# A hybrid encoder layer on one core: the moving operand of the last matmul stages in blocks of 512 columns, softmax by two heads a step

## What is computed

```python
D_MODEL = SEQ = 1024; BATCH = DEPTH = 1; N_MEM = 256; GROUP = 256; XATTN_HEADS = 4   # head width 256
def memory_cross_attention(h, mem_n, wq, wk, wv, wo):
    q = (h @ wq).reshape(B, T, XATTN_HEADS, XATTN_HEAD_DIM)
    k = (mem_n @ wk).reshape(B, M, XATTN_HEADS, XATTN_HEAD_DIM)
    v = (mem_n @ wv).reshape(B, M, XATTN_HEADS, XATTN_HEAD_DIM)
    s = jnp.einsum('bthd,bmhd->bhtm', q, k).astype(jnp.float32) * (XATTN_HEAD_DIM ** -0.5)
    p = jax.nn.softmax(s, axis=-1).astype(h.dtype)
    o = jnp.einsum('bhtm,bmhd->bthd', p, v).reshape(B, T, D_MODEL)
    return o @ wo
def reference(x, mem, ...):
        h = rms_norm(x, norm_mix[l])
        p = h @ w_in[l]                                   # 1024 -> 3904 columns
        p_a, p_b, p_c, p_d = jnp.split(p, splits, axis=-1)
        y_a = rwkv7_mixer(...)                            # delta-rule recurrence
        y_b = conformer_conv_mixer(...)                   # causal depthwise convolution, width 31
        y_c = hgrn2_mixer(...)                            # gated linear recurrence
        y_d = stick_breaking_mixer(...)                   # causal attention without softmax
        y = jnp.concatenate([y_a, y_b, y_c, y_d], axis=-1).astype(x.dtype)
        x = x + y @ w_out[l]
        hx = rms_norm(x, norm_xattn[l])
        mn = rms_norm(mem, norm_mem[l])
        x = x + memory_cross_attention(hx, mn, ...)
    return rms_norm(x, norm_final)
```

## Time and profile before

| | us |
|---|---|
| median of 3 runs | 1131.08 |
| lowest, highest | 1128.71, 1133.42 |
| span of the profiled execution, first to last instruction | 1128.3 |
| PE busy in it | 1058.6 (94%) |
| wide stages of the tail, first to last matmul | 822.5 to 1122.1 |
| of these, from the third block of the out projection on | 874.9 to 1122.1 |

### The profile page before, as it was taken

How to read it: one execution, slowest core, us unless ns; L and a number is a source line. 1 busy time by engine, 2 the same in 40 slices (tenths; PEclk the granted TensorE clock), 3 DMA queues, 4 the chain that set the end, 5 groups by cost and what they waited for, 6 DMA issues and landing times.

```text
span 1128.3 us, 25035 instructions
## 1 busy us (share of the span) xinstructions
PE 1058.6 (94%) x10748; PEld 915.3 (81%) x10748; DVE 576.8 (51%) x837; ACT 415.1 (37%) x719; POOL 288.5 (26%) x259
## 2 busy tenths in 40 slices
PE   6999978999899899989989799999989999999997
PEld 5788866886688698768868678888579999999997
DVE  6316998864447734153584875333231175445115
ACT  7314102023644411365534635555530062223033
POOL 3334640011326100113402000451142433422220
PEclk9999989999999999989989899999999999999999
DMA  7111110000111100021100017665551101111104
GB/s 236 36 31 47 47 47 3 3 22 20 30 28 47 29 4 3 2 75 39 39 20 20 2 42 216 200 186 163 193 180 38 48 31 46 58 47 39 38 20 150
DMA packets 83999, 71.16 MB, mean 63 GB/s; under 512 B 4081, under 2 KB 72881, under 8 KB 83890
## 3 DMA queue, kind: packets, MB, share of 16 engines
q1 hardware_dynamic: 83890, 69.57, 20.4%
HBM read 56.97 MB, written 12.58 MB: 62 GB/s over the span
## 4 chain that ended last, share of the span: by engine, by line
PE 69%; DVE 18%; ACT 7%; DMA 2%; issue 2%; POOL 1%; SPq 0%; DVEq 0%; ACTq 0%; POOLq 0%
PE units L1103 10%; PE bank L1372 7%; PE bank L1371 7%; PE bank L1373 7%; PE bank L1052 7%; PE bank L1054 6%; PE bank L1053 6%; DVE yT L1676 5%; PE bank L1092 5%; DVE A L1673 3%; ACT A L1392 2%; ACT B L1392 2%; PE duo L1319 2%; DVE late L1676 1%; PE duo L990 1%
## 5 line engine op out<-in xcount | busy, mean ns | idle before, releaser
L1371 PE MATMUL bank<-vhi,act_hi 128*128 128x256 f32 x704 | 200.4, 285 | 0.0
L1372 PE MATMUL bank<-vlo,act_hi 128*128 128x256 f32 x704 | 199.4, 283 | 0.0
L1373 PE MATMUL bank<-vhi,act_lo 128*128 128x256 f32 x704 | 198.1, 281 | 0.0
L1052 PE MATMUL bank<-act_hi,whi 128*128 128x512 f32 x464 | 192.7, 415 | 0.0
L1054 PE MATMUL bank<-act_hi,wlo 128*128 128x512 f32 x464 | 182.8, 394 | 0.0
L1053 PE MATMUL bank<-act_lo,whi 128*128 128x512 f32 x464 | 182.8, 394 | 0.0
L1103 PEld LDWEIGHTS units<-A 64*64 64x64 f32 x4608 | 147.1, 139 | 36.4 <-issue 18.3
L1103 PE MATMUL units<-A 64*64 64x64 f32 x4608 | 155.4, 224 | 22.3 <-DVE A L1839 9.7
L975 POOL TENSOR_SCALAR whi<-wraw 128x512 fp32r<-128x512 f32 x62 | 57.1, 922 | 456.5 <-PE bank L1054 388.4
L1372 PEld LDWEIGHTS bank<-vlo,act_hi 128*128 128x128 f32 x704 | 134.8, 192 | 0.0
L1373 PEld LDWEIGHTS bank<-vhi,act_lo 128*128 128x128 f32 x704 | 134.8, 191 | 0.0
(11 more groups left out here) (186 smaller groups left out, 1593.3 us busy)
## 6 DMA issues: line engine op xcount, KB each, us to landing
wraw<-in_w_in SPq DMA_DIRECT2D x62, 256.0 KB, 2.8
A<-in_x SPq DMA_DIRECT2D x8, 512.0 KB, 7.4
x<-in_x SPq DMA_DIRECT2D x8, 512.0 KB, 7.8
moved<-in_wq SPq DMA_DIRECT2D x16, 256.0 KB, 4.4
keys_dram<-moved SPq DMA_DIRECT2D x16, 256.0 KB, 2.1
vals_dram<-moved SPq DMA_DIRECT2D x16, 256.0 KB, 3.9
vraw<-in_w_out SPq DMA_DIRECT2D x16, 256.0 KB, 3.1
vraw<-keys_dram SPq DMA_DIRECT2D x16, 256.0 KB, 2.6
```

The costliest lines, as they stand in the source:

```text
L1052: mm(bank, wh, act_hi[:, k, cols], start=k == 0, stop=False)
L1371: mm(bank, ah, vhi[:, (m + 1) % 2, k, :], start=k == 0, stop=False)
L1372: mm(bank, ah, wide_lo(m)[:, k, :], start=False, stop=False)
L1373: ins = mm(bank, al, vhi[:, (m + 1) % 2, k, :], start=False, stop=k == KT - 1)
```

## The change

**The order of the mixers** is no longer planned. `mixer_order()` reads it from two tables, `TILE_ORDER` (the order of the projection's tiles) and `MERGE` (a string that says which chain moves next and how many steps). On every engine the instructions up to the sixteenth wide stage are the same ones in the same order as before; only the tail differs.

**The blocks of the wide stages** stand in a table `WIDES`. The out projection keeps two blocks of 256 columns and then has one of 512; scores and values have two of 512 each. A 512-column stage is again 24 matmuls, each with a moving operand of 128x512, and fills a whole bank. There are 56 wide stages in place of 96. Chunks are still 256 KB and 48 in number, but in a 512-column block one chunk is one slice k (128 rows of 2 KB), so a block takes 8.

**Places of the split operand.** The 512-column block of `o` lies in `o_rest`, on the memory of `yT`; POOL may write it once all eight `ysplit` are done. The four blocks of `s` and `f` go round 12 places of one slice each: eight in `vhi`/`vlo`, four in `vmore`, which lies on `ysp`. So the first four slices of a block have places of their own, and the last four take the places of slices of the block before. For these PE counts a new semaphore `v_used` in the last stage (i = 7) of a block, after slices 1, 3 and 5; POOL waits for it.

**Softmax** takes two heads a step: one maximum over 128x2x256, two exponentials, one reciprocal of two values, two multiplications. The final norm's two parts are 512 and 512 columns in place of 768 and 256.

```diff
+WIDES = (("o", 0, 0, 256), ("o", 1, 256, 256), ("o", 2, 512, 512),
+         ("s", 0, 0, 512), ("s", 1, 512, 512), ("f", 0, 0, 512), ("f", 1, 512, 512))
+WIDE_LOADS = [(m, k, HALF // w) for m, (_, _, _, w) in enumerate(WIDES) for k in range(0, KT, HALF // w)]
-IDLE = 24.099
...
+    for turn in MERGE.split():
...
-    s += [("wide", "o", n, i) for n in range(3) for i in range(2 if n < 2 else 0, TT)]
+    s += [("wide", "o", n, i) for n in range(2) for i in range(2, TT)]
     for i in range(TT):
-        s.append(("wide", "o", 3, i))
+        s.append(("wide", "o", 2, i))
         if i > 1:
             s.append(("hT", i - 2))
         s.append(("x2n", i))
-    for n in range(4):
+    for n in range(2):
         for i in range(TT):
             s += [("wide", "s", n, i), ("smax", n, i)]
...
-                pj.plan((name,) + a, reads=2 if a[0] == "s" else 1)
+                pj.plan((name,) + a, reads=3 if a[0] == "s" else 1)
...
+            if name == "o":
+                return o_rest[:, k, 0, :], o_rest[:, k, 1, :]
+            slot = (8 * (m - wide_at["s", 0]) + k) % 12
+            if slot >= 8:
+                return vmore[:, 0, slot - 8, :], vmore[:, 1, slot - 8, :]
+            return vhi[:, slot, :], (vlo0, vlo1)[slot // 4][:, slot % 4, :]
+
+        def wait_wide_place(eng, m, k):
...
+            elif name == "o" and n == 2 and k == 0:
+                eng.wait_ge(sem("y_split"), TT)
+            elif (name, n, k) == ("s", 0, 0):
+                pj.rd_open(eng, ("wide", "o", 1, TT - 1))
+            elif (name, n, k) == ("s", 1, 0):
+                pj.rd_open(eng, ("wide", "o", 2, 1))
+            elif name == "f" or (name, n) == ("s", 1) and k >= 4:
+                before = 8 * (m - wide_at["s", 0]) + k - 12
+                first, at = divmod(before, 8)
+                if at >= 6:
+                    pj.rd_open(eng, ("wide",) + WIDES[wide_at["s", 0] + first][:2] + (TT - 1,))
+                else:
+                    eng.wait_ge(sem("v_used"), 3 * first + at // 2 + 1)
...
-                bank = pj.pe_open(pe, key)[:, 0:256]
+                bank = pj.pe_open(pe, key)[:, 0:w]
                 for k in range(KT):
-                    if i == 0 and k % 2 == 0:
-                        pe.wait_ge(sem("v_split"), 4 * m + k // 2 + 1)
+                    if i == 0 and k % (HALF // w) == 0:
+                        pe.wait_ge(sem("v_split"), first + k // (HALF // w) + 1)
                     ah, al = hi[:, k, :], lo[:, k, :]
...
+                    mm(bank, ah, bh, start=k == 0, stop=False)
+                    mm(bank, ah, bl, start=False, stop=False)
+                    ins = mm(bank, al, bh, start=False, stop=k == KT - 1)
+                    if name != "o" and i == TT - 1 and k % 2 and k < KT - 1:
+                        ins.then_inc(sem("v_used"), 1)
```

More of the change, by code:

```diff
@@ L125, in mixer_chains, with step, halves @@
 def mixer_chains():
-    rec, stick, conv = [], [], []
+    rec, conv, stick = [], [], []
     def proj(*kind):
         return ("proj",) + kind + (1,)
-    def step(chain, stage, parts, *waits):
-        chain.append((stage, parts, ([chain[-1][0]] if chain else []) + list(waits)))
-    def halves(chain, stage, parts, waits=lambda h: None):
-        before = [chain[-1][0]]
+    def step(chain, stage, *needs):
+        chain.append((stage, ([chain[-1][0]] if chain else []) + list(needs)))
+    def halves(chain, stage, needs):
@@ L185, in mixer_chains @@
[L185 to L191 removed]
+            halves(rec, ("hlev", i, l), lambda h: [("hlev", i, l - 1, h) if l else ("hgate", i)])
@@ L211, in mixer_chains @@
                 if u:
[L212 removed]
+                    stick.append((("sbv", i, th, u - 1), [("sbt", i, th, u - 1)]))
                 if u < n:
[L214 to L225 removed]
@@ new lines, in mixer_chains, with cut @@
+                    stick.append((("sbt", i, th, u), [("sbz", i, th, u)]))
+            step(stick, ("sbo", i, th), proj("s", i, "gate"))
+    for i in range(2):
+        step(stick, ("ysplit", i), ("rfin", 1), ("hfin", 1), ("cfin",))
+    mem = [(("mn", 0), [("rfin", 1)]), (("mn", 1), []), (("mT", 0), [("mn", 0)]), (("mT", 1), [("mn", 1)])]
+    def cut(chain, *firsts):
+        at = [0] + [n for n, (stage, _) in enumerate(chain) if stage in firsts] + [len(chain)]
+        return [chain[a:b] for a, b in zip(at, at[1:])]
@@ new lines, in mixer_chains, with put @@
+    first, second, h0, h1 = cut(rec, ("lora", 1), ("hgate", 0), ("hgate", 1))
+    s0, s1 = cut(stick, ("sv", 1))
+    return {"a": first, "b": second, "g": h0, "h": h1, "c": conv, "s": s0, "t": s1, "m": mem}
+def mixer_order():
+    chains = mixer_chains()
+    pieces = [(t, 3, k) for t in (("xw",), FIRST_TILE) for k in range(KT)]
+    pieces += [(t, h, k) for t in TILE_ORDER for h, k in piece_list(t)]
+    order, placed = [], set()
+    def put(stage, needs=()):
+        assert all(n in placed for n in needs), (stage, needs)
+        order.append(stage)
+        placed.add(stage)
+    for turn in MERGE.split():
+        for _ in range(int(turn[1:] or 1)):
+            if turn[0] != "p":
+                put(*chains[turn[0]].pop(0))
+                continue
+            kind, h, k = pieces.pop(0)
+            put(("piece" if h < 2 else "part",) + kind + (h, k))
+            if k == max(piece_list(kind))[1]:
+                put(("proj",) + kind + (min(h, 1),))
+    assert not pieces and not any(chains.values())
@@ L931, in _ @@
                 sem("gain_loaded"), 16)
-            load_wides(2, 12)
+            for u in range(8, len(WIDE_LOADS)):
+                load_wide(u)
             for i in range(TT):
```

400 lines of the change are left out of this document (117 added, 283 removed), and 23 rows, old and new, of tables (MERGE, TILE_ORDER, TILE_RANK).

## The result

| | before | after |
|---|---|---|
| median (lowest to highest) of the runs taken together, us | 1132.33 (1128.71 to 1133.42) | 1124.11 (1122.31 to 1126.10), 5 runs |
| ratio, with its 95% interval | | 0.9939 (0.9918 to 0.9959) |
| span of the profiled execution | 1128.3 | 1120.5 |
| first 512-column stage, start | 874.85 | 876.29 |
| from there to the last matmul ("the tail" below) | 247.22 | 237.60 |

One run of before that lay far off (1940 us) is left out of the range; it is one of the five behind the median, which without it is 1131.7. Two later measurements of the same changed kernel gave 1121.73 us (8 runs) and 1122.05 us (6 runs). All 19 runs together have a median of 1122.4 us, and 52 runs of before, from all the comparisons of this study and without the one of 1940 us, 1132.5 us.

What follows compares the result with a forecast made beforehand. PE was taken to bound the kernel; -12.8 (matmuls) - 3.3 (stalls) + 0.6 (supply) + 0.3 (end) = -15.2 us carried the median of 1131.08 to 1115.9 us. Range 1112.5 to 1120, to 1122 with one slow boundary.

Steps and rivals of the forecast that it cites:

- The bound and the part that doesn't change: Whole kernel: PE alone sets the tail's end at clock 1.00; the 875 us before it keep their time.
- Matmuls, -12.8: Tail: 1920 matmuls of 256 columns become 960 of 512 at 0.2267 us each, 12.8 us less.
- the rival that the fixed part is not halved: Tail matmuls: the 13 ns are not tied to the instruction, pairing saves nothing, 1128.7 us; chance 0.05.
- Stalls at the transposes, -3.3: Out projection's normalized rows: PE's two waits at transposing groups go away, 3.3 us less.
- Supply, +0.6: Second scores and second values blocks: PE waits 0.3 us at each for late slices, 0.6 us more.
- The prediction's bound: Supply at three boundaries: with splits of up to 2.14 us a chunk, up to about 10 us more.
- POOL falls behind at one boundary: One block boundary: slow splits cost PE 3.4 us and a lower clock 1.7, giving 1121.0 us; chance 0.07.
- the lower clock it had feared: Behind a PE wait for POOL: 1.2 GHz for 3.4 us, costing 1.7 us, part of the slow boundary rival.
- Banks, clock, end: Tail: no waits for scores banks, clock 1.00 throughout, DVE's last addition 0.3 us longer.
- The rival of a lower clock in dense work: Tail: denser column feeding lowers PE's clock; 45 us at 1.2 GHz give 1138 us; chance 0.03.
- The sum: Whole kernel: -12.8 - 3.3 + 0.6 + 0.3 = -15.2 us, giving 1115.9 us.
- The stated range: Whole kernel's time: 1112.5 to 1120 us, reaching to 1122 with one slow boundary and holding some 0.85.

Runs made afterwards that it cites:

- align256_deep: Changed kernel with pads of 256 bytes, giving all operands the remainder 128 modulo 256, and four landing buffers in place of two; 1117.29 us, ratio 0.9848 to the kernel before.
- the best kernel: The kernel `align256_deep`: pads of 256 bytes and four landing buffers added to the changed kernel; 1117.29 us, tail 232.24 us.
- shift: Changed kernel with 96 more already met wait instructions at the start of PE's program, to move instruction fetches against the loads; 1128.92 us (one run).
- misalign: Changed kernel with the pad of 32 bytes moved in front of `vhi`, so `vhi` and `vlo0` get remainder 160 too; 1123.17 us (one run).

## Why the prediction was wrong, step by step

**The bound and the part that doesn't change.** Right. PE alone sets the end, the clock is 1.00, and the sixteen stages and mixers ahead kept their time within what executions differ by.

**Matmuls, -12.8.** The mechanism held and its size was off. A fixed part of about 13 ns does belong to the instruction: with matching places a matmul of 512 columns costs 0.2267 us in the dense stages of every block (`align256_deep`), as the mixers' stretch said, and the rival that the fixed part is not halved is out. The step that failed is the carrying over of that distance to all 40 stages. In the mixers' stretch `act_hi` stood against `wlo` and `whi`, tensors at the remainder 128 like itself. In the kernel after, all 32 stages of scores and values have four or eight of their slices in `vmore` or `vlo1`, and two more have `ysp` standing still. With four landing buffers in both, the places make 235.18 - 232.24 = 2.9 us. The stages of before could not have shown it: at 256 columns the distance is 0.1200 in blocks with `vlo1` too.

By the formula of the Trainium skill for an isolated matmul (TensorE: Matmul & The Clock Gate, section Back-to-back issue gap) the step would have been 2.4 us, an estimate. By the runs it gives 12.8 where places agree and 9.9 where they don't, so a fixed part of 2.5 ns is not what this kernel pays.

**Stalls at the transposes, -3.3.** Right. All 16 groups stand 0.79 to 0.80 us ahead of the next stage, and PE waits at none.

**What wasn't priced.** A stage behind a transposing group is longer than a dense one, by 0.12 us with 512 columns where it was 0.07 with 256. Sixteen of these are 0.8 us more. The other 0.3 lie in single slices elsewhere: some in before took less than 0.360 (down to 0.349, most of them in the out projection), and a few in the best kernel more than 0.680. That is why the best kernel's tail is 232.24 and not 231.1 (the 231.7 of the steps less the 0.6 that four buffers save).

**Supply, +0.6.** The likeliest value was wrong; the place was right. The second scores block lost 0.5 us (0.3 forecast). The second values block lost 2.0 (0.3 forecast), 0.4 of it as in `shift`, where the loads ran undisturbed, and the rest because the last load took twice its time with a fetch in it. The prediction's bound came from the row of the longest *split*, 2.14 us, and looked for a slower POOL. It was the *load*, whose landing times stand in the same group of rows, that was late: 4.3 us where 2.7 is the median. The 7.1 us there is no measure of it, since that load was issued at 833.4, in the crowded second block of the out projection (DMA share 0.93). In the tail of before the slowest took 3.6, and 4.8 in its second trace. The sum took the median, where the slowest of the late loads sets the wait. The rival "POOL falls behind at one boundary" came near in its place and size (3.4 forecast, 2.0 measured), with the wrong cause (that its time of 1121.0 us lies so near the measured one is chance, since it has no term for the places), and without the lower clock it had feared: PE's clock is 1.00 behind the 1.71 us of waiting.

**Banks, clock, end.** Right: no wait for DVE or ACT, 1.00 throughout, and the end 0.4 us longer (0.3 forecast). The rival of a lower clock in dense work is out.

**The sum.** Tail: 231.7 forecast, 237.6 measured. The difference of 5.9 is 2.9 for places, 1.8 for the boundaries (2.4 less the 0.6 forecast) and 1.1 that wasn't priced. Put on the forecast of 1115.9 us, it gives 1121.8, near the median of 1122.4 of all 19 runs. The stated range ended at 1122, so 1121.8 is just inside, the 19 runs 0.4 us above it, and the 1124.11 of the first measurement 2.1 above it; the 1.7 us between these two are less than executions differ by ahead of the tail. The range was too narrow because it took one stretch of 10 us as the price of 40 stages without a term for what differed there, the tensors.

## What to carry to other kernels

Put the operands of long runs of wide matmuls at the same byte address modulo 256, since one odd pad cost up to 3% of each of them here, and compare the median lengths of one instruction by tile to find such a pad. Where a change takes cover away from a supply, price it by the slowest load of that stretch, not by the median, and look for idle rows that nothing explains in the engine that now becomes tight, also where they cost nothing before. A distance taken from another stretch holds for the tensors of that stretch.

## What the runs showed of the hardware

- **Places of operands.** A slice of three matmuls with 128x512 moving operands takes 0.680 us when moving and standing operands share the address modulo 256. It takes about 0.70 with a difference of 32 bytes, and from 0.68 to 0.70 with 64 or 128 bytes. With 256 columns, in dense stages of scores and values, it is 0.360 us either way. `misalign` shows that it is the moving against the standing operand. The extra cost does not stop with the odd tensor: in the kernel after, the slices in `vhi` that follow four in `vmore` still take 0.694 and 0.690, then 0.680. Open is why one odd tensor among the three matmuls (`vlo1`) costs nearly as much per slice as three (`vmore`), and why 64 and 128 bytes cost different amounts from slice to slice. The Trainium skill (SBUF — State Buffer, section Operand start alignment) asks only for a start at a multiple of the element size, and says its runs timed nothing; no case here was off it.
- **Instruction fetches among the loads.** A packet of 16 KB comes every 25 to 31 us of the tail after. The load of 256 KB before it took 1.3 us from its first packet to its last (1066.99 to 1068.25), the one that it fell into 2.9 (1069.08 to 1071.98), with one engine of sixteen busy at the end, from the moment the 16 KB packet was through.
- **A transposing group slows the matmul behind it**, by 0.08 us where the moving operand has 512 columns (0.31 from the start at 938.30 to the next, where 0.23 is usual). With 256 its length is 0.36 in place of 0.28.
